# Turning attention probabilities by a diagonal of inverse sums, with a new order of tiles in the hyena and C layers of a four-layer diffusion backbone

## The reference

```
def _dense_block_attention(q, k, v, scale):          # A: 8 heads, 2 of keys, 128 wide
    s = einsum(q, k) * scale; p = softmax(s); return einsum(p, v)
def _window_attention(...):                          # C: 16 heads, 2 of keys, 64 wide, a sink logit a head
    p = softmax([sink, s_ctx, masked s_loc])[1:]; return p_ctx @ v_ctx + p_loc @ v_loc
def _hyena_mixer(h, ...):                            # B
    x0, x1, v = split(dwconv(h @ w_in + b_in))
    v = long_conv(v * x1) + skip;  return (v * x0) @ w_out + b_out
h = h + gate * rmsnorm(mixer(u), g1);  h = h + gate * rmsnorm(ffn(u), g3)
```

## Time and profile before

| | us |
|---|---|
| median of 3 runs (lowest, highest) | 2288.19 (2286.65, 2290.29) |
| the profiled execution | 2291.39 |
| its span | 2289.6 |

### The profile page before, as it was taken

The page is one execution under the profiler, slowest core; times in us unless marked ns, Lnnn a source line. Parts: engine busy times, 40 slices in busy tenths (PEclk is TensorE's granted clock), DMA queues, the critical chain, the costliest instruction groups (busy, mean ns, idle before and its releaser), DMA issues.

```text
span 2289.6 us, 28755 instructions
## 1 busy us (share of the span) xinstructions
PE 2175.4 (95%) x11688; PEld 1767.1 (77%) x11688; DVE 1437.8 (63%) x2212; ACT 884.0 (39%) x1329; POOL 217.5 (9%) x253
## 2 busy tenths in 40 slices
PE   5999999999999988899999999999999999998998
PEld 3877888888787756788888787478888878868996
DVE  2426558887756532667887754866787776655553
ACT  3327443332244311443332243854333223455543
POOL 0000011110010014111110001100111100100110
PEclk7999999999999999999999999999999999999999
DMA  9460335546532210334546532022454563214554
GB/s 308 141 209 19 111 101 161 171 150 217 194 126 83 83 37 19 102 100 158 166 149 220 202 103 65 1 84 82 149 165 156 184 211 120 99 45 131 185 182 140
DMA packets 224745, 304.98 MB, mean 133 GB/s; under 512 B 6738, under 2 KB 153243, under 8 KB 224486
## 3 DMA queue, kind: packets, MB, share of 16 engines
q1 hardware_dynamic: 220541, 290.11, 39.0%
q0 software_dynamic: 3664, 12.87, 1.7%
q10 hardware_dynamic: 409, 0.16, 0.0%
HBM read 302.00 MB, written 1.11 MB: 132 GB/s over the span
## 4 chain that ended last, share of the span: by engine, by line
PE 78%; DVE 10%; ACT 5%; DMA 3%; issue 2%; SPq 1%; POOL 1%; ACTq 0%; DVEq 0%; POOLq 0%
PE lo L639 16%; PE lo L640 16%; PE lo L641 16%; PE lo L705 4%; PE lo L706 4%; PE lo L707 4%; DVE w_lo L1383 2%; ACT w_hi L1059 2%; PE lo L973 2%; PE hi L705 2%; PE hi L707 2%; PE hi L706 2%; DMA w_raw<-in_ffn_w_down 1%; PE hi L986 1%; PE stat L705 1%
## 5 line engine op out<-in xcount | busy, mean ns | idle before, releaser
L639 PE MATMUL lo<-u_hi,w_hi 128*128 128x512 f32 (+1 forms) x2072 | 736.5, 355 | 9.0 <-DVE w_lo L1383 3.8
L640 PE MATMUL lo<-u_lo,w_hi 128*128 128x512 f32 (+1 forms) x2072 | 723.2, 349 | 0.0
L641 PE MATMUL lo<-u_hi,w_lo 128*128 128x512 f32 (+1 forms) x2072 | 722.6, 349 | 0.0
L1383 DVE TENSOR_TENSOR w_lo<-w_raw,w_hi 128x2048 fp32r<-128x2048 f32 (+1 forms) x182 | 406.7, 2235 | 356.9 <-ACT w_hi L1059 355.7
L1059 ACT ACTIVATE w_hi<-w_raw 128x2048 fp32r<-128x2048 f32 (+1 forms) x182 | 339.5, 1867 | 478.9 <-DMA w_raw<-in_ffn_w_down 266.7
L639 PEld LDWEIGHTS lo<-u_hi,w_hi 128*128 128x128 f32 x2072 | 394.7, 191 | 74.1 <-issue 19.3
L641 PEld LDWEIGHTS lo<-u_hi,w_lo 128*128 128x128 f32 x2072 | 394.5, 190 | 50.1
L640 PEld LDWEIGHTS lo<-u_lo,w_hi 128*128 128x128 f32 x2072 | 394.7, 190 | 49.7 <-issue 1.2
L1400 DVE SCALAR_TENSOR_TENSOR mod_acc<-mod_raw,silu_c,mod_acc 128x512 f32<-128x512 f32 x504 | 394.6, 848 | 9.9 <-DMA mod_raw<-in_mod_w 9.9
L1912 POOL TENSOR_TENSOR mid_lo<-conv,mid_hi 128x512 fp32r<-128x512 f32 (+1 forms) x88 | 117.8, 1359 | 1055.7 <-ACT mid_hi L1362 1055.7
L705 PE MATMUL lo<-w_hi,mid_hi 128*128 128x512 f32 x374 | 147.4, 394 | 3.7 <-DVE u_raw L1450 2.6
(11 more groups left out here) (296 smaller groups left out, 2698.2 us busy)
## 6 DMA issues: line engine op xcount, KB each, us to landing
w_raw<-in_ffn_w_up SPq DMA_DIRECT2D x88, 1024.0 KB, 5.1
mod_raw<-in_mod_w SPq DMA_DIRECT2D x144, 512.0 KB, 4.0
w_raw<-in_ffn_w_down SPq DMA_DIRECT2D x40, 1024.0 KB, 5.1
mod_unit<-in_mod_w SPq DMA_DIRECT2D x24, 1024.0 KB, 6.8
w_raw<-in_a_w_qkv SPq DMA_DIRECT2D x12, 1024.0 KB, 5.2
w_raw<-in_b_w_in SPq DMA_DIRECT2D x12, 1024.0 KB, 5.1
w_raw<-in_a_w_out SPq DMA_DIRECT2D x8, 1024.0 KB, 5.1
w_raw<-in_ffn_w_down SPq DMA_DIRECT2D x8, 512.0 KB, 3.6
```

Of the source, the lines that this page charges most:

```text
L639: mm(o, h3[:, k, c], x, start=(first and k == 0), stop=False)
L640: mm(o, h3[:, k, c], y, start=False, stop=False)
L641: ins = mm(o, l3[:, k, c], x, start=False, stop=(last and k == nr - 1))
L1383: tt(WL[:, n % 3, 0:words], RAW[:, n % 3, 0:words], WH[:, n % 3, 0:words].bitcast(F32), ALU.subtract).then_inc(lo_ready, 1)
```

## The change

1. **Turns.** normalise no longer touches the probabilities. It writes the identity scaled by the inverse sums into a ring of eight 128x128 diagonals (inv_sum, in the place of squares), one for kinds 0 and 1, two for kind 2, and waits until the turn that last read the slot is done. turn multiplies each block of unscaled probabilities by the diagonal instead of transposing it.
2. **Hyena.** fill() is gone: all out tiles follow the last inverse.
3. **C layer.** The second weight tile is query chunks 2 and 3 (full width) and the third is the keys (half width), before it was the other way round. The first turns are those of queries 0 and 1 in tile 2; queries 2, 3 and both key turns stand in tile 3.
4. **Out phases.** A root of a constant, whose result nobody reads, follows the squares of the first half in each phase. In the mixers' phases of layers 1 and 2 the low part of the next weight tile (lo(L + 1)) moves from block 0 to behind the diagonal of block 1.

```diff
...
     else:
-        TILES += [("c_w_qkv", _j, 0, KT, 0, TW), ("c_w_qkv", _j, 0, KT, D, P)]
-        TILES += [("c_w_qkv", _j, 0, KT, TW * t, TW) for t in range(1, 4)]
+        TILES += [("c_w_qkv", _j, 0, KT, TW * t, TW) for t in range(2)]
+        TILES += [("c_w_qkv", _j, 0, KT, D, P)]
+        TILES += [("c_w_qkv", _j, 0, KT, TW * t, TW) for t in range(2, 4)]
         TILES += [("c_w_qkv", _j, 0, KT, D + P, P)]
...
-      2: [[0, 1], [8], [2, 3], [4, 5], [6, 7], [9]],
+      2: [[0, 1], [2, 3], [8], [4, 5], [6, 7], [9]],
...
-TURNS = {0: [8, 9, 0, 1, 2, 3, 4, 5, 6, 7], 2: [8, 9, 0, 1, 2, 3, 4, 5, 6, 7], 3: [0, 1, 8, 9, 2, 3, 4, 5, 6, 7]}
+TURNS = {0: [8, 9, 0, 1, 2, 3, 4, 5, 6, 7], 2: [0, 1, 2, 3, 8, 9, 4, 5, 6, 7], 3: [0, 1, 8, 9, 2, 3, 4, 5, 6, 7]}
...
-           2: {2: {0: [0], 2: [1], 4: [2], 6: [3]}, 3: {2: [4], 5: [5]}, 4: {2: [6], 5: [7]}, 5: {1: [8], 3: [9]}},
+           2: {2: {0: [0], 4: [1]}, 3: {0: [2], 2: [3], 4: [4], 6: [5]}, 4: {2: [6], 5: [7]}, 5: {1: [8], 3: [9]}},
...
         SQ = place("squares", [P, 2, TOK])
+        RD = place("inv_sum", [P, 8, P], at=SQ_AT)
...
-        R1 = place("inv_o", [P, 2, 4])
+        R1 = place("inv_o", [P, 2, 5])
...
+        ND = {i: [sum(1 if t < 2 else 2 for h, t in HALVES[i][:x]) for x in range(NH[i] + 1)] for i in ATT}
...
                         for b in range(1 if t < 2 else 2):
                             at = kt * (1 if t < 2 else 2) + b
                             src = kt * P if t < 2 else (CTX if A else CTX + 4) * b + kt * P
-                            last = nc.tensor.transpose(t_bank(i, x)[:, at * P:(at + 1) * P], p[:, src:src + P], ident)
+                            last = mm(t_bank(i, x)[:, at * P:(at + 1) * P], p[:, src:src + P], RD[:, (ND[i][x] + b) % 8, :],
+                                      start=True, stop=True)
...
-            def long_conv(fill):
+            def long_conv():
...
                     if w < 3:
                         forward(w + 1)
-                    else:
-                        fill()
                     inverse(w)
...
-                    long_conv(lambda: x_tiles(2, UH, UL, arrive, free, [0]))
...
                 for b in range(NB):
                     o_square(k, 0, b)
+                f(R1[:, 1, 4:5], eps[:, :], ACT.Sqrt)
...
-                    if b == 0:
+                    if b == 0 and not has_bias(k):
                         lo(L + 1)
...
                     if more and not (b == 1 and NB == 2):
                         diagonal(k + 1, b)
+                    if b == 1 and has_bias(k):
+                        lo(L + 1)
...
-                    sl, p = small[:, x % 6, :, :], PB[:, x % 6, :]
+                    sl = small[:, x % 6, :, :]
                     dve.wait_ge(s_exp, G + x + 1)
+                    free = [y for y in range(x) if ND[i][y] <= ND[i][x + 1] - 9]
+                    if free:
+                        dve.wait_ge(p_turned, G + free[-1] + 1)
                     link(nc.vector.reciprocal(sl[:, 3, 0:nb], sl[:, 2, 0:nb]))
                     for b in range(nb):
-                        c0 = b * (CTX if A else CTX + 4)
-                        s = slice(c0, c0 + TOK // nb)
-                        ins = ts(p[:, s], p[:, s], sl[:, 3, b:b + 1], None, ALU.mult)
+                        ins = ts(RD[:, (ND[i][x] + b) % 8, :], ident, sl[:, 3, b:b + 1], None, ALU.mult)
                     ins.then_inc(s_norm, 1)
```

More of the change, by code:

```diff
@@ L695, in u_turns, with x_phase @@
                     last.then_inc(u_turned, 1)
-            def x_tiles(k, X, Y, arrive, free, ts, end=False):
+            def x_phase(k, X, Y, arrive, free):
                 n0, nt, NB = XFIRST[k], XTILES[k], XN[k]
@@ L719, in finished @@
                         ins.then_inc(x_done, 1)
-                for t in ts:
+                for t in range(2 * nt - 2):
                     n, (h, tt) = n0 + t, divmod(t, nt)
@@ L752, in x_tiles @@
                 n = n0 + 2 * nt - 2
-                for b in range(NB if end else 0):
+                for b in range(NB):
                     if nt == 2:
@@ L1011, in _ @@
                         filter_stage(t)
+                    long_conv()
                     arrive = lambda k: pe.wait_ge(c_lo, 8 * (k // 4 + 1))
                     free = lambda b: ((c_prod, 32),)
-                    long_conv(lambda: x_tiles(2, UH, UL, arrive, free, [0]))
                 else:
@@ L1037, in _ @@
                     free = lambda b, i=i: ((p_evac, ahead(NH, i) + NH[i]),) if b < 2 else ((ao_lo, ahead(GROUPS, i) + GROUPS[i] - 3 + b),)
-                x_tiles(2 * i, UH, UL, arrive, free, range(KIND[i] == 1, 2), end=True)
+                x_phase(2 * i, UH, UL, arrive, free)
                 n0, q0 = FIRST["up", i], PAIR0["up", i]
@@ L1044, in _ @@
                     tile(n0 + t, q0 + t, N, UH, UL, True, True)
-                x_tiles(2 * i + 1, MH, ML, lambda k, b=i * FM: pe.wait_ge(ml_ready, b + k + 1),
-                        lambda b, q=q0 + FM: (released(q - 2 + b // 2),), range(10), end=True)
+                x_phase(2 * i + 1, MH, ML, lambda k, b=i * FM: pe.wait_ge(ml_ready, b + k + 1),
+                        lambda b, q=q0 + FM: (released(q - 2 + b // 2),))
         @block.scalar
@@ L1947, in QCOS @@
 def QCOS(i, j):
-    return sum(10 if KIND[k] == 0 else 8 for k in range(i) if KIND[k] != 1) + (j if KIND[i] == 0 else j - 2)
+    return (sum(10 if KIND[k] == 0 else 8 for k in range(i) if KIND[k] != 1)
+            + sum(KIND[i] == 0 or r < 8 for r in TURNS[i][:j]))
 _INS = ["x", "c", "ctx", "c_ctx", "mod_w", "mod_b", "norm_g", "ffn_w_up", "ffn_conv_w", "ffn_conv_b", "ffn_w_down",
```

## The result

The changed kernel takes 2301.91 us (median of 4 runs, 2300.83 to 2303.77) beside 2289.24 for the kernel before in the same comparison (4 runs). The ratio is 1.0057, with an interval of 1.0040 to 1.0074: slower by 13 us (9 to 17), where +8.1 was forecast. The profiled execution took 2300.83 (span 2299.0).

A forecast was written before the change was run, and what follows sets the result against it. TensorE, busy for 95% of the span, was taken as the bound. Turning +19.6 (39.6 - 17.7 - 2.3), hyena tail -5.9, opening -5.5 and out phases -0.1 gave +8.1 us, median 2296.3, range 2286 to 2310.

The forecast's parts named there:

- the likeliest case: Whole kernel: slower by +8.1 us, median 2296.3; the forecast itself has a chance of 0.61.
- The turn's price: Attention layers 0, 2 and 3: a half's turn costs TensorE 0.89 instead of 0.44 us, +39.6 us over 88 halves.
- the fourfold case: Rival, attention turns: a half takes 1.76 us, the rest as forecast, +84 us, 2373; chance 0.01.
- What the waits absorb: Attention layers: TensorE's waits for VectorE absorb 17.7 us of longer turns, 12.5 in layer 2, 2.5 and 2.7 elsewhere.
- Hyena tail: Hyena layer's end: tile 0 covers the 6.26 us wait, a 2.0 us wait is new; -5.9 us, between -7.2 and -4.
- opening: C layer's start: the 3.55 us key wait and its half clock go; -5.5 us, between -6.2 and -3.
- The margin of 2 us: Hyena out tiles: third following tile's raw load, 5.1 us to land, is ready at 927; tile 1 ends at 929.
- the thing late next: Hyena out tiles: the third following out tile's raw load, starting 9 us later at tile 0's end.
- The out phases: All eight out phases: earlier root table, later weight split in layers 1 and 2; sum -0.1 us, between -2.5 and +3.
- the first gap's gain of 2 us: Out phases of layers 1 and 2: diagonal comes 2 us earlier, gaps of 2.36 us shrink to about 0.5.
- The half clock as a whole: Given back: 2.3 us at the turns, 2.4 at the hyena tail, 2.7 at the opening; 0.8 new before the inverse.

The follow-up runs named there:

- the run with the early loads: The changed kernel with GpSimd's loads of the hyena layer's out bias, gate scratch and gates moved ahead of its last gate steps: 2301.68 us, 1.0060 against the kernel before.

## Why the prediction was right, and where it was off

**The sign and the likeliest case** held: +13 us (9 to 17) against +8.1, inside 2286 to 2310.

**The turn's price** held. 704 records, 0.90 us a half instead of 0.44. The Trainium skill's rule (TensorE: Matmul & The Clock Gate, Terms, the row on the xbus) that the transpose mode is four times as fast for FP32 doesn't fit this chip's rows: both forms stand at a ratio of two (0.44 and 0.90 us a half), and the fourfold case would have shown +84 us.

**What the waits absorb** held in kind and was too hopeful in layer 2. By sections, with the first two halves of layer 2 counted there, the growth is 7.5, 10.8 and 4.0 us, 22.3 in all, where the working gives 7.1, 8.2 and 4.5, 19.8. Layer 2's 10.8 is also just above the 7 to 10 that the prediction named as its sign. 21.6 us of longer products came to 10.8, and the clock there rose from 0.98 to 1.00 over some 93 us, which is 1.9 us: so its waits gave back about 9 us, where I took 12.5. The weight loads' waits did fall by 11.8 (14.5 to 2.7), but weight loads run beside products, and the products themselves had waited only 6.6 us for VectorE in this stretch (1.0 now).

**Hyena tail and opening** held by themselves: -6.0 and -7.6 (section -5.5) against -5.9 and -5.5 (the first by its own terms is 6.6 less 0.85, -5.75). The margin of 2 us that I left for the third tile's raw load was too small: it took 5.1 us to land for granted, while GpSimd's gate loads stand at the same place. The prediction named the thing late next and missed what it would share the transfer engines with. In the profiled execution that cost the first gap's gain of 2 us, 1.4 of which the new wait behind it would have taken anyway, as the run with the early loads shows. In both together, without the turning, the two gave 3 us more than forecast (-14.6 against -11.4).

**The out phases** held: +0.9 (-1.4 to +3.2) against -0.1. In layer 1 TensorE waits 2.61 us for the last row block where it was 0.46, as the text said, and the wait of 1.43 us between the two was not foreseen; in layer 2 the last wait was 2.08 us already before. The root follows the table's load at once here as well, so no drain was missed (the Trainium skill, ScalarE: Activation LUTs, What ACT_TABLE_LOAD costs, adds 1.38 us). ScalarE's timeline of the changed kernel:

```profile
945.34 1.28 ACT L1122 ACT_TABLE_LOAD   x1
946.64 0.20 ACT L1122 ACTIVATE inv_o<-eps 128x1 f32<-128x1 f32 x1
```

**Where the 5 us between +8.1 and +13 lie.** The forecast is just below the measured interval (9 to 17). The table has 2.5 us in the attention layers (22.3 for 19.8): the term of the waits that TensorE's longer turns absorb in layer 2, about 9 us for 12.5, is the step that was mis-sized. Another 2.5 us lie between 827 and 975, where the changed kernel has gained 3.4 us (-5.6 + 2.2) and the forecast has 5.9. TensorE's waits at the turns of h there are 5.2 us, where they were 2.8 before. With the out phases' part alone they are 4.4, by the wait of 1.43 us that the prediction lacked; the other 0.8 goes with the raw load that landed late. These places are read from one execution of each kernel, to about 1 us each. The half clock as a whole was not off: 2.3, 2.4 and 2.7 us were counted as given back and 0.8 as new, 6.6 in all, and the mean clocks give 45.0 - 39.1 = 5.9. But it isn't where it was counted, since each stretch was taken from one execution of the kernel before as if it belonged to its gap.

**Some of the agreement is luck.** Measured alone, the four parts are 20.6 - 6.0 - 7.6 + 0.9 = +7.9, which looks like the forecast's 8.1 term by term. From the runs of more parts at once the same sum is +5.5 (20.6 - 15.1) or +6.0 (20.6 - 14.6), and measured together they are 13. Each of these sums carries some 5 us of noise. The forecast added its parts as if they were independent, and they aren't quite: they share half clock, and the turning with the moved tile brings two loads together that meet with neither alone. The gaps of 6.26 and 3.55 us are gone from every trace with these edits; the half clock that they win back differs from trace to trace.

## What to carry to other kernels

Moving work from an engine that is 63% busy to the one that is 95% busy pays only what the busy one had been waiting for, and that can be read beforehand: 39.6 us of products, less 17.7 of waits and 2.3 of half clock, was to give 19.6, and it gave 20.6. The price of the two forms of a turn stood in the old trace already, in another stage. Before a load is moved later, look at what other queues start at the same moment. And of several edits that each remove a gap, count the idle time fully, but don't add up the half clock that each wins back alone.

## What was not expected of the hardware

Of two loads that meet, the one that started second paid. A 1 MB load took 9.1 us instead of 5.0 when it started 0.6 us behind two of 512 KB from GpSimd's queue (927.28 and 926.64), which took 6.0 us. It took 5.0 when it started 0.8 us ahead of them (918.93 and 919.74, hyena tail and opening), and they took 7.9.

The half clock behind a gap isn't a property of the gap. At the same place in the opening, 3.55 us of idle came with a mean clock of 0.72 over 12 us, 3.71 us in another kernel with 1.00, and 3.56 us in a third with 0.72 again.
